# FFN 1's up projection by Strassen in two groups of F, and the modulation in 512-column units beside the down blocks

## What is computed

```
c_act = silu(c);  mod = c_act @ w_ada + b_ada          # 9 sections of 1024: shift, scale, gate x 3
x = x + 0.5 * gate1 * SwiGLU_1(modulate(rms(x)))       # FFN 1: (silu(h Wg) * (h Wu)) W_out
x = x + gate2 * W_out [pool mixer ; gMLP mixer]        # mixer, from modulate(rms(x)) @ w_mix_in
x = x + 0.5 * gate3 * SwiGLU_2(modulate(rms(x)))       # FFN 2
y = rms(x) * gain
```

## Time and profile before

| what | us |
|---|---|
| median of 3 runs | 887.66 (887.58 to 889.74) |
| the profiled execution | 887.46 |
| its span | 885.7 |
| PE busy | 858.6 (97%) |
| DVE busy | 584.3 (66%) |
| ACT busy | 331.7 (37%) |
| mean DMA rate | 152 GB/s |

### The profile page before, as it was taken

The page is one execution under the profiler, slowest core; times in us unless marked ns, Lnnn a source line. Parts: engine busy times, 40 slices in busy tenths (PEclk is TensorE's granted clock), DMA queues, the critical chain, the costliest instruction groups (busy, mean ns, idle before and its releaser), DMA issues.

```text
span 885.7 us, 13665 instructions
## 1 busy us (share of the span) xinstructions
PE 858.6 (97%) x5290; PEld 744.6 (84%) x5290; DVE 584.3 (66%) x902; ACT 331.7 (37%) x434; POOL 36.0 (4%) x42
## 2 busy tenths in 40 slices
PE   4899999999999999999999999999999999999997
PEld 3678888888888888897887898899988899999886
DVE  4579777777777756538645469988633588885443
ACT  6232222222223221225424356666521256655223
POOL 0000000000000000000340000000000000100000
PEclk9899999999999999999999999999999999999998
DMA  9978666666667555434533322576343476663322
GB/s 273 287 199 244 189 190 191 190 190 191 192 179 207 168 164 174 146 104 110 144 95 95 94 74 72 135 178 171 83 131 94 117 185 159 151 155 91 98 66 95
DMA packets 219483, 134.44 MB, mean 152 GB/s; under 512 B 5560, under 2 KB 214572, under 8 KB 219436
## 3 DMA queue, kind: packets, MB, share of 16 engines
q1 hardware_dynamic: 216500, 128.52, 50.8%
q0 software_dynamic: 2880, 5.24, 3.6%
q10 hardware_dynamic: 56, 0.01, 0.0%
HBM read 126.41 MB, written 2.10 MB: 145 GB/s over the span
## 4 chain that ended last, share of the span: by engine, by line
PE 90%; DVE 6%; ACT 2%; SPq 1%; DMA 1%; issue 1%; ACTq 0%
PE ps L1558 22%; PE ps L1560 21%; PE ps L1559 21%; PE ps L1935 7%; PE ps L1931 7%; PE ps L1933 7%; DVE h_lo L1010 1%; PE ps L1813 1%; PE ps L1814 1%; PE ps L1815 1%; DMA w_raw<-in_ffn_w_in_dram 1%; PE ps L1749 1%; DVE sw_lo_a L1436 1%; DVE w_split L968 1%; DVE xs L1003 0%
## 5 line engine op out<-in xcount | busy, mean ns | idle before, releaser
L1558 PE MATMUL ps<-h_hi,w_split 128*128 128x512 f32 (+1 forms) x464 | 182.4, 393 | 8.8 <-DVE h_lo L1010 8.6
L1560 PE MATMUL ps<-h_hi,w_split 128*128 128x512 f32 (+1 forms) x464 | 179.2, 386 | 0.0
L1559 PE MATMUL ps<-h_lo,w_split 128*128 128x512 f32 (+1 forms) x464 | 178.0, 384 | 0.0
L957 DVE TENSOR_TENSOR w_split<-w_raw,w_split 128x2048 fp32r<-128x2048 f32 (+1 forms) x45 | 93.3, 2073 | 76.6 <-ACT w_split L601 76.6
L1558 PEld LDWEIGHTS ps<-h_hi,w_split 128*128 128x128 f32 x464 | 87.9, 189 | 27.9 <-issue 6.0
L601 ACT CAST w_split<-w_raw 128x2048 fp32r<-128x2048 f32 (+1 forms) x45 | 77.1, 1712 | 81.2 <-PE ps L1560 72.8
L1560 PEld LDWEIGHTS ps<-h_hi,w_split 128*128 128x128 f32 x464 | 87.7, 189 | 19.1
L1559 PEld LDWEIGHTS ps<-h_lo,w_split 128*128 128x128 f32 x464 | 87.8, 189 | 17.5
L1054 DVE SCALAR_TENSOR_TENSOR ada_acc<-ada_raw,c_act,ada_acc 128x256 f32<-128x256 f32 x196 | 95.0, 485 | 7.0
L1931 PE MATMUL ps<-sums_hi,sw_hi 128*128 128x256 f32 x320 | 89.6, 280 | 0.9 <-DVE sw_lo_a L1436 0.5
L1933 PE MATMUL ps<-sums_lo,sw_hi 128*128 128x256 f32 x320 | 89.8, 281 | 0.0
(11 more groups left out here) (186 smaller groups left out, 1532.6 us busy)
## 6 DMA issues: line engine op xcount, KB each, us to landing
ada_raw<-in_w_ada_dram SPq DMA_DIRECT2D x56, 512.0 KB, 3.7
sw_raw<-in_ffn_w_in_dram SPq DMA_DIRECT2D x100, 256.0 KB, 4.1
w_raw<-in_ffn_w_in_dram SPq DMA_DIRECT2D x48, 512.0 KB, 6.1
ada_first<-in_w_ada_dram SPq DMA_DIRECT2D x16, 512.0 KB, 7.4
w_raw<-in_ffn_w_out_dram SPq DMA_DIRECT2D x16, 384.0 KB, 4.0
w_raw<-in_w_mix_in_dram SPq DMA_DIRECT2D x12, 512.0 KB, 4.4
sw_raw<-in_ffn_w_out_dram SPq DMA_DIRECT2D x16, 384.0 KB, 4.1
w_raw<-in_ffn_w_out_dram SPq DMA_DIRECT2D x16, 320.0 KB, 3.3
```

The costliest lines, as they stand in the source:

```text
L957: nc.vector.tensor_tensor(w_lo[s][:, 0:n], w_raw[s][:, 0:n], w_hi[s][:, 0:n].bitcast(F32), ALU.subtract).then_inc(lo_ready, 1)
L1558: nc.tensor.matmul(dst, w_h, a_h, start=start, stop=False)
L1559: nc.tensor.matmul(dst, w_h, a_l, start=False, stop=False)
L1560: return nc.tensor.matmul(dst, w_l, a_h, start=False, stop=stop)
```

## The change

- FFN 1's up projection: 8 plain steps (`PLAIN = (8, 2)`), then 14 tiles by Strassen, 3 in group 0 and 11 in group 1, with the code of FFN 2. Its down projection is done per group, in 8 + 8 blocks of 33 matmuls. The sums of h for FFN 1 are made in plain steps 2 and 3. Semaphores of the scheme exist once for each FFN.
- `sw_raw` lies over `ada_raw`, so `ada_raw` can't be used while FFN 1 runs on Strassen items. A down block's raw weights fill 1408 of the 3584 columns of its slot; the rest now carries ("hosts") half a unit of w_ada.
- The modulation's units are 512 columns wide, 14 of them, each in two parts of 4 k-tiles (1 MB): 28 parts. Parts 0 to 3 run in plain steps 0, 1 and 4, parts 4 to 17 are hosted by blocks 0 to 6 of both groups of FFN 1, parts 18 to 23 run in the mixer out of `ada_raw`, parts 24 to 27 are hosted by blocks 0 to 3 of FFN 2's group 0.
- The v weights of the mixer get buffers of their own and are loaded after block 4's load of group 1.

```diff
+    PLAIN = (8, 2)
+    ADA_PLAIN = {0: (0,), 1: (1,), 4: (2, 3)}
+    ADA_MIX = tuple(range(18, 24))
+    HOSTED = ({down_item(0, g, m): 4 + 7 * g + m for g in range(2) for m in range(7)},
+              {down_item(1, 0, m): 24 + m for m in range(4)})
+    TAKES = ((0, 2), (2, 8), (8, 12), (12, 13), (13, 14))
+    def used(part, steps=KD // 2):
+        return part // 2 * LINKS + part % 2 * (KD // 2) + steps
...
 SP
+            def sw_free(f, i):
+                if i < 2:
+                    ...
+                else:
+                    sp.wait_ge(sw_lo_ready[f], pieces(f, i - 1))
+                    if i - 2 in HOSTED[f]:
+                        sp.wait_ge(ada_link, used(HOSTED[f][i - 2]))
+            def load_down2(f, g, m):
+                i = down_item(f, g, m)
+                s = i % 2
+                sw_free(f, i)
+                to = sw_raw[:, s, 0:DN].rearrange("p (k n) -> p k n", n=P)
+                for k0, k1 in ((0, GF // 2), (GF // 2, GF)):
+                    sp.dma_start(...).then_inc(sw_full[f][s], 16)
+                if i in HOSTED[f]:
+                    part = HOSTED[f][i]
+                    k0 = part % 2 * KA
+                    sp.dma_start(host_view(s), w_ada_v[:, k0:k0 + KA, ada_cols(part)])\
+                      .then_inc(host_full[f][s], 16)
+            for m in range(KD):
+                load_down2(0, 1, m)
+                if m == KD - 4:
+                    sp.wait_ge(sw_used[0], pieces(0, up_item(0, NS[0] - 1) + 1))
+                    for kq in range(2):
+                        load_v(w_mix_in, kq)
...
 ACT, group 1 of FFN 1
+            for m in range(KD - 1):
+                cast_down(0, 1, m + 1)
...
+                square(m, 0)
+            split_hi(MIXIN)
...
 DVE
+            def ada_steps(part, raw_of, full_of):
+                u, k0 = part // 2, part % 2 * KA
+                acc, turned = work[:, 3, :], work[:, 4, :]
+                for q in range(KA):
+                    k = k0 + q
+                    if u or k:
+                        dve.wait_ge(ada_link, u * LINKS + k)
+                    full, count = full_of(q)
+                    dve.wait_ge(full, count)
+                    (k == 0: tensor_scalar, else scalar_tensor_tensor, 512 columns)
+                    ins.then_inc(ada_link, 1)
+                if part % 2:
+                    (transpose, reduce_sum, 512 columns)
+            for m in range(KD):                      # FFN 1, group 0
+                if m == 0:
+                    product_of(0, N0[0] - 1)
+                    product_rest(0, N0[0] - 1)
+                if m < KD - 1:
+                    rest_down(0, 0, m + 1)
+                else:
+                    add_blocks(0, N0[0])
+                    rest_up(0, N0[0], 0)
+                if m == 0:
+                    take_mod(0)
+                    half_gates(0, 0, KD, 1)
+                if down_item(0, 0, m) in HOSTED[0]:
+                    ada_hosted(0, down_item(0, 0, m))
+                update_part(0, m)
+            up_group(0, 1)
+            for m in range(KD - 1):                  # FFN 1, group 1
...
+                rest_down(0, 1, m + 1)
+                if m == KD - 2:
+                    take_mod(1)
+                    gains(1, "gmix", 4)
+                    dve.wait_ge(mod_ready, 2)
+                ada_hosted(0, down_item(0, 1, m))
+                update_last(0, m)
+                add_squares(X_AT[0] + m + 1)
+            split_lo(MIXIN)
...
+            ada_own(18)                              # mixer, between the splits of MIXIN + 2 and + 3
+            ada_own(19)
             split_lo(MIXIN + 3)
...
             split_lo(MIXOUT)
+            ada_own(20)
+            ada_own(21)
...
+                if m == 0:                           # FFN 2, group 0, after rest_down(1, 0, m + 1)
+                    ada_hosted(1, down_item(1, 0, 0))
+                    ada_hosted(1, down_item(1, 0, 1))
+                else:
+                    if m == 1:
+                        take_mod(3)
+                        half_gates(1, 0, KA, 4)
+                        update_part(1, 0)
+                    if m == 3:
+                        take_mod(4)
+                        half_gates(1, KA, KD, 5)
+                    if m in (1, 2):
+                        ada_hosted(1, down_item(1, 0, m + 1))
+                    update_part(1, m)
...
 PE
-            up(UP1, 0)
-            down(DOWN1, 0, X_AT[0], SQ_AT[0], False, beside).then_inc(chunk_done, 1)
+            plain(0, 2)
+            for j in range(3, PLAIN[0]):
+                pair(j % 2, UP1 + j, (2 * (j % 2), 2 * (j % 2) + 1), h_hi, h_lo)
+            for n in range(N0[0]):
+                strassen(0, n)
+            sum_units(0)
+            for m in range(KD):
+                down2(0, 0, m)
+            for n in range(N0[0], NS[0]):
+                strassen(0, n)
+            for m in range(KD - 1):
+                if m == KD - 2:
+                    sum_units(1)
+                down2(0, 1, m)
+            down2_half(KD - 1, 0)
+            pe.wait_ge(mod_link, 2 * (P // Q))
+            sum_blocks(KD)
+            down2_half(KD - 1, 1, beside)
+            (FFN 2: sum_units(3), sum_units(4) inside down blocks 1 and 3 of group 0, at k = 6)
```

More of the change, by code:

```diff
@@ L731, in copy_out @@
                 nc.scalar.copy(out_tok[:, :, bass.ds(m * P, P)], src).then_inc(out_copied, 1)
-            def down(base, x_count, sq_count, last):
-                nc.scalar.activation(dummy, ones[:, 0:1], ACT.Sqrt)
-                with act.Fori(0, KD - 1) as m:
-                    for s in range(2):
-                        split_hi(s, HALF, (m * 2 + (base + s + 2), m + (base // 2 + 1)))
-                    square(m, m + x_count, m + (sq_count + 1))
-                    if last:
-                        copy_out(m)
-                if not last:
-                    split_hi(0, FULL, base + 2 * KD)
-                act.wait_ge(sq_added, sq_count + KD)
@@ L1039, in take_mod, with half_gates @@
                         .then_inc(mod_link, 1)
-                dve.wait_ge(mod_link, n * (P // Q))
-            def ada_unit(u):
-                for k in range(KD):
-                    if not (isinstance(u, int) and u == 0 and k == 0):
+                dve.wait_ge(mod_link, (n + 1) * (P // Q))
+            def half_gates(f, k0, k1, n):
+                at = (3 * NORM_OF[f] + 2) * KD
+                nc.vector.tensor_scalar(half_gate[:, f, k0:k1], mod[:, at + k0:at + k1], -HALF_STEP, None, ALU.mult)\
+                    .then_inc(mod_ready, 1)
+                dve.wait_ge(mod_ready, n)
@@ L1526, in _ @@
-            for n in range(N0):
-                up_slot(n)
+            split_lo_part(UP2 + 1, 0)
+            hsum_1(1)
+            split_lo_part(UP2 + 1, 1)
+            add_blocks(1, 0)
+            plain_product(1, 0)
+            hsum_rest(1, 0)
+            rest_up(1, 0, 0)
+            hsum_3(1)
+            hsum_2(1)
+            rest_up(1, 0, 1)
+            hsum_rest(1, 2)
+            hsum_rest(1, 1)
+            hsum_4(1)
+            rest_up(1, 0, 2)
+            plain_lo(1, 0)
+            hsum_rest(1, 3)
@@ new lines, in half_product @@
+            def half_product(j, dst, src_hi, src_lo, start, stop):
+                w_h, w_l = sw_block(sw_hi, j), lo_block(j)
+                for k in range(KA):
+                    nc.tensor.matmul(dst, w_h[:, k, :], src_hi[:, k, :], start=start and k == 0, stop=False,
+                                     skip_group_check=True)
+                    nc.tensor.matmul(dst, w_h[:, k, :], src_lo[:, k, :], start=False, stop=False,
+                                     skip_group_check=True)
+                    ins = nc.tensor.matmul(dst, w_l[:, k, :], src_hi[:, k, :], start=False,
+                                           stop=stop and k == KA - 1, skip_group_check=True)
+                return ins
@@ new lines, in down2_half @@
+            def down2_half(m, half, between=None):
+                cols = HALVES[half]
+                hi, lo = (v.rearrange("p (k n) -> p k n", n=P) for v in (down_hi(m), down_lo(m)))
+                for k in range(GF):
+                    if between:
+                        between(k)
+                    ins = product(ps[:, LAST_BANK[half], cols], hi[:, k, :], lo[:, k, :], b_hi[:, k, cols],
+                                  b_lo[:, k, cols], k == 0, k == GF - 1)
+                ins.then_inc(last_done, 1)
@@ L2015, in transposes @@
+            for n in range(N0[1], NS[1]):
+                strassen(1, n)
             def transposes(k):
```

1373 lines of the change are left out of this document (627 added, 746 removed).

## The result

The changed kernel takes **939.82 us** (median of 4 runs, 938.31 to 941.54) against 887.67 before: a ratio of 1.0572 (95% interval 1.0547 to 1.0596), slower. The profiled execution has a span of 937.9 us against 885.7. Forecast were 930, 908 to 945, and slower with 0.90. Sign and mechanism came out; the sum was 9 us short, 7.8 of it in one term, the mixer.

What follows compares the result with a forecast made beforehand. PE, busy 97% of the span, was taken to bound the kernel. Savings of 15.1 us against added seams, ring, clock, mixer and FFN 2 waits summed to +42.9 us, giving 930.5 us, range 908 to 945.

Steps and rivals of the forecast that it cites:

- Tiles: FFN 1's up projection: 14 Strassen tiles at 9.90 us replace plain steps at 10.98, -15.1 us.
- seams: FFN 1's switches between up and down work: up to down twice, down to up once, about 0.6 each, +1.8 us.
- clock: After the 5.7 us wait before group 1's up tiles, PE runs 3.4 us at half pace, +1.7 us.
- Ring, group 0: FFN 1's group 0 down blocks: part, load, cast, split go round in 10.6 us against PE's 7.56, +17.1 us.
- the way to the up tiles: From FFN 1's group 0 to tile 3: its load waits for block 6's part, so PE idles, +5.7 us.
- Ring, group 1: The same round in FFN 1's group 1 down blocks, one landing later behind v-weight loads, +18.5 us.
- Seam to the mixer: End of FFN 1 to v tiles: part 17 delays sum of squares and v-weight split, 17.1 against 10.4, +6.7 us.
- Mixer: In the mixer, parts 18 and 19 delay LN's statistics, part 21's late load a split; +3.6 us, bounds 0 and 8.
- FFN 2: FFN 2's blocks 0 to 3 host parts; waits for unit 12 and before block 2, together +2.9 us, 6 at most.
- the load is not held: FFN 1's down blocks: part done before SP's wait, so only seams and mixer are paid; 879 us, 9% chance.
- The load lands sooner: FFN 1's down blocks: loads land at the shortest 3.2 us, 12 rounds 0.9 shorter each; 919 us, 9% chance.
- The clock doesn't come back: FFN 1's down blocks: each 3 us idle puts the whole next block at the lower clock; 970 us, 3% chance.

Runs made afterwards that it cites:

- run 9: On top of run 8: group 0 of FFN 1 hosts 8 parts, group 1 only 6; some parts, waits and v-weight loads moved; 878.60 us.
- run 1: Changed kernel, but SP's load of a down block waits only for the split, no longer for its modulation part; 901.54 us.
- run 2: Changed kernel with SP's waits kept, but DVE does block m's part ahead of the split for block m + 1; 900.56 us.
- run 3: Changed kernel, but parts hosted in FFN 1's down blocks multiply only 16 of 512 columns, modulation incomplete; 915.76 us.
- run 6: Changed kernel with only part 21's load moved: own place, issued behind part 20's; 931.95 us.
- run 7: Changed kernel with the first two pairs, ws_raw and parts 18 and 19 loaded ahead, parts 20 and 21 unmoved; 932.50 us.
- run 4: Changed kernel with the mixer's loads moved earlier (first two pairs, ws_raw, parts 18 to 21), DVE's work and order kept; 925.88 us.
- run 8: Changed kernel with the edits of run 1 and run 4 together; 891.60 us, 1.0035 of the kernel before.

## Why the prediction was right, and where it was short

- **Tiles (-15.1) and seams (+1.8), clock (+1.7)**: right. The 5.88 us of waiting before the up tile were followed by 4.1 us at 0.50, where the forecast had 3.4. 14 tiles with their seams changed by -12.4, against -11.6. In run 9, where one wait of 1.05 is left at the seam into group 1, they gave -14.8 (139.0 in place of 153.8).
- **Ring, group 0 (+17.1) and the way to the up tiles (+5.7)**: 23.7 against 22.8. Round 10.65 against 10.6; the up tile waited 5.88. (Two sums of the prediction are rounded low: its terms give 9.7 and 2.3 us, not 9.6 and 2.1, for block 2, and 5.9, not 5.7, for the up tile.) Runs 1 and 2 cut the round at either end and lost it; run 3 shortened one link and the round followed.
- **Ring, group 1 (+18.5)**: 18.2, with 3.73 in the block behind the v loads.
- **Seam to the mixer (+6.7)**: 7.9. The wait for the sum of squares was not one of 4 but 2.25 for the sum and 1.38 for the last squares. The clock was at 0.50 before it (422.2 to 425.4) and again from 432.4 to 439.0, 0.73 over the stage; this second stretch lies in the way from `update_half` to the v tiles, which took 7.4 (433.38 to 440.79) where the forecast took over 5.4.
- **Mixer (+3.6, bounds 0 to 8)**: this is the step that failed, at 11.4, over its upper bound. Its own terms add up to 5.5 (6.6 less 5 of cover, and 3.9); for taking 3.6 it gives no reason. Three errors. First, part 21's load was seen, but its price was read off the split at 476.71. Ahead of this split in DVE's order stands y_lo, for which PE waits; in DVE's timeline of the kernel before:

```profile
472.47 3.21 DVE L1313 SCALAR_TENSOR_TENSOR y_lo<-ps,vcol,y_hi 128x512 fp32r<-128x512 f32 x4 [7.47 <-ACT y_hi L788]
```

  With the forecast's landing at 474, the part (3.1) with its transpose and sum (1.4) ends near 478.5, which puts y_lo 6.0 later, by an estimate; moving the load gave 6.6 (run 6). Counted from the first v tile, y_lo stood at 70.3 us before and at 81.7 after: these 11.5 are the mixer's loss. Second, of the 6.6 for part 19's late load 5 were taken as cover; this load with part 18's and ws_raw's was worth 6.7 (run 7). Third, ws_raw was no term at all, though SP issues it behind part 18's load (PE waited 1.62). The upper bound took DVE's work less the cover as the worst case; with the loads in time this work costs 0.3 (run 4), and with late loads DVE idles 11.6 us beside it. That the time stayed under 945 with this term 3.4 over its bound is owed to the other terms, which left their part of the range unused.
- **FFN 2 (+2.9)**: the down group that hosts took 3.1 more (63.6 against 60.5), 2.0 of it in the two waits named (1.1 and 0.9). That the whole came to 2.2 is a group of tiles that took 0.9 less (109.4 against 110.4), with the same code.
- **Rival "the load is not held"**: it is what run 1 builds. It had 879 for the kernel so freed; that kernel takes 901.5, and with the mixer's loads in time as well (run 8) 891.6, since seams and tail kept their waits; with most of these gone it is 878.6. **"The load lands sooner"**: it landed 4.65 after the first issue, as taken. The Trainium skill's formula (page "DMA: Bandwidth & Descriptors", section "Anatomy of one DMA") would have had 2.9, an estimate, for the second DMA, where the median landing was again 4.1; the page gives it for DMAs issued from GpSimd, and this one is issued from SP.
- **"The clock doesn't come back"**: not as a whole block at the lower level, but a low stretch could be longer than the 3.4 us that I carried over from the earlier trace rows, 5.8 us in one block (below).

## What to carry to other kernels

Work put into a spare part of a slot is not free when the slot's next load waits for it: follow the round release, load, cast, split, work, and compare it with the block's length. A load that shares no bytes with that work should not wait behind it in the queue. Where new work goes ahead of old on an engine, look at the first old instruction behind it that someone waits for, and at when its data is loaded: here late loads cost 11 us and the work itself 0.3.

## What the runs showed that I had not expected

Equal waits of PE had unequal effects on its clock. Windows of the changed kernel; two blocks of the ring that both began after a wait of about 3 us (3.03 and 2.91):

```profile
184.20:186.20 2.00, 2.00 (x5) 1.61 (x6) 1.89 (x4) 0.00 (x0) 0.00 (x0) 0.50 0.05 19
188.20:190.20 2.00, 2.00 (x7) 1.57 (x6) 0.00 (x0) 0.00 (x0) 0.00 (x0) 0.56 0.98 290
190.20:191.70 1.50, 1.50 (x8) 1.25 (x7) 0.00 (x0) 0.23 (x1) 0.00 (x0) 1.00 0.98 290
205.40:207.40 2.00, 2.00 (x9) 1.66 (x10) 1.89 (x4) 0.00 (x0) 0.00 (x0) 1.00 0.03 8
```

The first ran 5.8 us at 0.50 (1.2 GHz) and took 10.4 us, just under the round; the second ran at 1.00 (2.4 GHz) and then waited 2.8. Either way the next block began 10.4 to 10.7 later, so within the ring the clock cost nothing. Outside it, it did: in run 8 the waits of 1.4 and 2.4 before the up tile were followed by 3.3 us at 0.50, an estimated 1.7 us lost, and with one wait of 1.05 in their place (run 9) there was no low stretch. Why equal waits differ so stays open. And an operation of DVE on 16 columns took 0.26 us where 512 took 0.78: a third of the price for a thirty-second of the work.
